# Attention of a streaming encoder: sample values by head on half columns, equal units together, key copies on two engines, both scores taken ahead of the second scaling

## What is computed

```python
# fox: every query block sees all keys up to itself, with a forget term
s = einsum('bqhd,bkhd->bhqk', q_blk, k_all) * ATTN_SCALE
s = s + cq_blk[..., None] - c[:, :, None, :]
s = where(k_pos <= q_pos, s, NEG_INF)
o = einsum('bhqk,bkhd->bqhd', softmax(s), v_all)
# band: a chunk of 64 sees itself and 8 chunks before, with a relative bias
s = einsum('bnqhd,bnkhd->bnhqk', q_ch, k_band) * ATTN_SCALE
s = where(valid, s + bias, NEG_INF)
o = einsum('bnhqk,bnkhd->bnqhd', softmax(s), v_band)
mix = concatenate([o_fox, o_lru, o_band]) @ W_out
```

## Time and profile before

| | |
|---|---|
| three runs, us | 1543.34, 1542.04, 1546.4 (median 1543.34) |
| the profiled execution, us | 1543.2, of which its span is 1541.5 |
| TensorE, VectorE, ScalarE, GpSimd busy, share of the span | 95%, 47%, 30%, 6% |
| attention, from the first key turn to the first matmul of the output projection | 303.1 to 514.7 us of the span |
| chain that ended last, by engine | TensorE 89%, VectorE 6%, ScalarE 2%, issue 1%, DMA 1% |

### The profile page before, as it was taken

The page is one execution under the profiler, slowest core; times in us unless marked ns, Lnnn a source line. Parts: engine busy times, 40 slices in busy tenths (PEclk is TensorE's granted clock), DMA queues, the critical chain, the costliest instruction groups (busy, mean ns, idle before and its releaser), DMA issues.

```text
span 1541.5 us, 20612 instructions
## 1 busy us (share of the span) xinstructions
PE 1461.6 (95%) x8470; PEld 1325.3 (86%) x8470; DVE 728.2 (47%) x1216; ACT 458.4 (30%) x671; POOL 90.7 (6%) x129
## 2 busy tenths in 40 slices
PE   6999999978888899999999999999999999999994
PEld 6999979855666688989898989898989999999993
DVE  6433621166667555553536353535353535444336
ACT  6353332054446543412121212121212221212123
POOL 3000003211000002000000000000000000000006
PEclk9999999989999999999999999999999999999998
DMA  6210212225021323311010111101010101111033
GB/s 206 83 31 35 97 58 108 87 70 190 15 83 55 124 86 106 98 54 55 28 54 27 54 43 39 54 27 54 27 54 27 54 27 54 36 46 52 16 116 135
DMA packets 80005, 102.87 MB, mean 67 GB/s; under 512 B 3592, under 2 KB 63237, under 8 KB 79806
## 3 DMA queue, kind: packets, MB, share of 16 engines
q1 hardware_dynamic: 71744, 73.43, 15.4%
q0 software_dynamic: 8208, 28.69, 5.4%
HBM read 85.52 MB, written 16.58 MB: 66 GB/s over the span
## 4 chain that ended last, share of the span: by engine, by line
PE 89%; DVE 6%; ACT 2%; issue 1%; DMA 1%; POOL 0%; SPq 0%; ACTq 0%; DVEq 0%
PE PS L1423 49%; PE PS L1743 18%; PE PS L1492 7%; PE PS L1710 6%; PE PS L1413 3%; PE PS L1559 2%; PE PS L1665 1%; PE PS L1652 1%; DVE f_acc L1396 1%; DVE probs L1209 1%; PE PS L1498 1%; DVE kt_s L1186 1%; DVE f_acc L1369 1%; PE PS L1582 0%; DMA x_in<-in_x_prompt 0%
## 5 line engine op out<-in xcount | busy, mean ns | idle before, releaser
L1423 PE MATMUL PS<-act_hi,w_hi 128*128 128x384 f32 x1152 | 208.4, 334 | 0.0
L1423 PE MATMUL PS<-act_hi,w_lo 128*128 128x384 f32 x1152 | 207.9, 334 | 0.0
L1423 PE MATMUL PS<-act_lo,w_hi 128*128 128x384 f32 x1152 | 207.9, 334 | 0.0
L1423 PEld LDWEIGHTS PS<-act_hi,w_hi 128*128 128x128 f32 x1152 | 200.8, 188 | 0.9
L1423 PEld LDWEIGHTS PS<-act_hi,w_lo 128*128 128x128 f32 x1152 | 200.4, 188 | 0.0
L1423 PEld LDWEIGHTS PS<-act_lo,w_hi 128*128 128x128 f32 x1152 | 200.4, 188 | 0.0
L1369 DVE TENSOR_TENSOR f_acc<-f_acc,PS 128x512 f32<-128x512 f32 x216 | 145.5, 686 | 77.8 <-PE PS L1743 77.8
L1743 PE MATMUL PS<-w_hi,f_hi 128*128 128x512 f32 x432 | 168.8, 391 | 5.4 <-ACT ffn_rows L977 5.4
L1743 PE MATMUL PS<-w_hi,f_lo 128*128 128x512 f32 x432 | 168.4, 390 | 0.0
L1743 PE MATMUL PS<-w_lo,f_hi 128*128 128x512 f32 x432 | 168.3, 390 | 0.0
L899 ACT ACTIVATE w_hi<-raw 128x1024 fp32r<-128x1024 f32 x72 | 72.1, 1049 | 225.2 <-PE PS L1743 219.5
(11 more groups left out here) (326 smaller groups left out, 2002.9 us busy)
## 6 DMA issues: line engine op xcount, KB each, us to landing
raw<-in_w_up SPq DMA_DIRECT2D x48, 512.0 KB, 4.7
raw<-in_w_down SPq DMA_DIRECT2D x24, 512.0 KB, 3.9
raw<-in_w_in SPq DMA_DIRECT2D x18, 512.0 KB, 4.6
x_scratch<-x POOLq DMA_DIRECT2D x9, 512.0 KB, 5.0
x_back<-x_scratch SPq DMA_DIRECT2D x1, 4608.0 KB, 14.2
x_in<-in_x_prompt SPq DMA_DIRECT2D x8, 512.0 KB, 5.9
raw<-in_w_out SPq DMA_DIRECT2D x8, 512.0 KB, 3.6
x_res<-in_x_prompt SPq DMA_DIRECT2D x8, 512.0 KB, 4.1
```

The lines of the kernel that those rows point to most:

```text
L1423: last = pe.matmul(PS[0:width, banks + c, 0:CW], w(wp, k), acts[ap][:, k, c * CW:(c + 1) * CW], start=(n == 0 and k == 0), stop=(n == 2 an ...
```

## The change

Five things are done together.

- The order of units: fox blocks now come as 5, 7, 6, 4, 3, 2, 1, 0 (before 7, 0, 6, 1, 5, 2, 4, 3), band blocks as 4, 3, 5, 2, 6, 1, 7, 0. Key and sample units stand at given places among them, and the two sample units of a kind no longer follow each other: fox samples at units 21 and 23 (before 22 and 23), band samples at 32 and 37 (before 34 and 35). The splits of output weights begin at unit 37 (before 36) and wait for the scores of the last band sample unit, not for its values.
- Key copies: the second step of a key unit is copied by ScalarE (`take_keys`), the first by VectorE. `scores_used` becomes two semaphores, one for each step.
- VectorE takes both scores of unit m + 2 ahead of the second scaling of unit m + 1.
- Sample values: before, a product gave 128 rows (two heads) by 64 columns (the probabilities of all four heads), of which each head's rows used 16 columns. Now each head has its own product of 64 rows by 16 columns on one half of the array's columns, and the new frames' part is one product of 32 columns for both streams.
- The sample output is copied by one instruction in place of four.

```diff
+        out = []
+        for n in range(len(units) + 1):
+            out += [turn for turn, at in turns if at == n] + units[n:n + 1]
+        return out
...
+    among_fox = list(zip(pairs_of("kb") + pairs_of("kt") + pairs_of("sf"), (9, 11, 12, 14, 15, 16)))
+    among_band = list(zip(pairs_of("kt") + pairs_of("sb"), (4, 5, 6, 10)))
+    units = pairs_of("kf") + with_turns(among_fox, fox) + with_turns(among_band, band)
...
-FOX_ORDER = (7, 0, 6, 1, 5, 2, 4, 3)
-BAND_ORDER = (4, 0, 5, 1, 6, 2, 7, 3)
+FOX_ORDER = (5, 7, 6, 4, 3, 2, 1, 0)
+BAND_ORDER = (4, 3, 5, 2, 6, 1, 7, 0)
...
-OUT_SPLITS = [LAST["sb"] // 2 + 1 + q for q in range(6)]
+OUT_SPLITS = [LAST["sb"] // 2 + q for q in range(6)]
...
+            def take_keys(n):
+                dst, w = keys_of(n)
+                act.wait_ge(scores_ready, n + 1)
+                act.activation(dst, PS[:, 2:4, :].rearrange("p b c -> p (b c)")[:, 0:w], ACT.Copy)\
+                   .then_inc(scores_used[1], 1)
...
                 if q == 0:
-                    act.wait_ge(att_out, outputs_until(LAST["sb"]))
+                    act.wait_ge(scores_ready, LAST["sb"] + 1)
...
+            take_keys(1)
+            take_keys(3)
             for m in range(NUNIT):
...
                 if is_real(m + 2):
                     exponent(2 * (m + 2))
+                elif m + 2 < NUNIT:
+                    take_keys(2 * (m + 2) + 1)
...
                 if m + 2 < NUNIT:
                     take_scores(2 * (m + 2))
+                if is_real(m + 2):
+                    take_scores(2 * (m + 2) + 1)
                 if is_real(m + 1):
                     normalise(COUNT[2 * (m + 1) + 1])
-                if m + 2 < NUNIT:
-                    take_scores(2 * (m + 2) + 1)
...
-                    pe.wait_ge(scores_used, 2 * m + s - 1)
+                    pe.wait_ge(scores_used[s], m)
...
-                                for k in range(3):
-                                    vals = cache_v[:, b, k, t * P:(t + 1) * P] if k < 2 else new[:, NPT, t * P:(t + 1) * P]
-                                    last = pe.matmul(PS[:, bank, c0:c0 + 64], vals,
-                                                     turned[:, k * P + 64 * b2:k * P + 64 * b2 + 64],
-                                                     start=k == 0, stop=k == 2)
+                                for k in range(2):
+                                    for g in range(2):
+                                        col = k * P + 64 * b2 + TS * (2 * t + g)
+                                        pe.matmul(PS[64 * g:64 * g + 64, bank, c0 + TS * b2:c0 + TS * (b2 + 1)],
+                                                  cache_v[:, b, k, t * P + HD * g:t * P + HD * (g + 1)],
+                                                  turned[:, col:col + TS], start=(s, t, b2, k) == (0, 0, 0, 0),
+                                                  stop=False, skip_group_check=True)
+                            for g in range(2):
+                                last = pe.matmul(PS[64 * g:64 * g + 64, bank, c0:c0 + 2 * TS],
+                                                 new[:, NPT, t * P + HD * g:t * P + HD * (g + 1)],
+                                                 new_probs[:, :, 2 * t + g, :], start=False, stop=True,
+                                                 skip_group_check=True)
```

More of the change, by code:

```diff
@@ L133, in with_turns @@
     def with_turns(turns, units):
-        mixed = [x for p, turn in enumerate(turns) for x in (turn, units[p])]
-        return mixed + units[len(turns):]
+        out = []
+        for n in range(len(units) + 1):
+            out += [turn for turn, at in turns if at == n] + units[n:n + 1]
+        return out
     fox, band = prompt("pf", FOX_ORDER), prompt("pb", BAND_ORDER)
-    units = (pairs_of("kf") + fox[:9] + with_turns(pairs_of("kb") + pairs_of("kt"), fox[9:]) + pairs_of("sf")
-             + band[:4] + with_turns(pairs_of("kt"), band[4:8]) + pairs_of("sb") + band[8:])
+    among_fox = list(zip(pairs_of("kb") + pairs_of("kt") + pairs_of("sf"), (9, 11, 12, 14, 15, 16)))
+    among_band = list(zip(pairs_of("kt") + pairs_of("sb"), (4, 5, 6, 10)))
+    units = pairs_of("kf") + with_turns(among_fox, fox) + with_turns(among_band, band)
     return [sub for u in units for sub in u]
-FOX_ORDER = (7, 0, 6, 1, 5, 2, 4, 3)
-BAND_ORDER = (4, 0, 5, 1, 6, 2, 7, 3)
+FOX_ORDER = (5, 7, 6, 4, 3, 2, 1, 0)
+BAND_ORDER = (4, 3, 5, 2, 6, 1, 7, 0)
 STEPS = attention_steps()
@@ L489, in probs_t_of, with keys_of @@
             return ring(r, probs_t, 1)
+        def keys_of(n):
+            st = STEPS[n]
+            if st[0] == "kt":
+                return kt_s[:, 2 * st[1]:2 * st[1] + 2, :, :].rearrange("p b t c -> p (b t c)"), 1024
+            cols, w = (slice(0, SEQ), SEQ) if st[1] < 2 else (slice(SEQ, T), P)
+            return (kt_f if st[0] == "kf" else kt_b)[:, st[1] % 2, cols], w
         def turned_x(t):
@@ L859, in exponent @@
                 r = COUNT[n]
-                act.wait_ge(scores_used, n + 1)
+                act.wait_ge(scores_used[n % 2], n // 2 + 1)
                 p_r = probs_of(r)[:, 0:widths(n)]
@@ L1237, in take_output @@
                     c0 = SEQ + 2 * TS * st[1]
-                    out = PS[:, bank, :].rearrange("p (s t b c) -> p s t b c", s=2, t=2, b=2)
-                    for h in range(H):
-                        t, rows = h // 2, slice(64 * (h % 2), 64 * (h % 2) + 64)
-                        last = dve.tensor_copy(
-                            mix[rows, tile0 + t, c0:c0 + 4 * TS].rearrange("p (s b c) -> p s b c", s=2, b=2),
-                            out[rows, :, t, :, TS * h:TS * (h + 1)])
-                    last.then_inc(att_out_used, 1)
+                    dve.tensor_copy(
+                        mix[:, tile0:tile0 + 2, c0:c0 + 4 * TS].rearrange("p t (s x) -> p s t x", s=2),
+                        PS[:, bank, 0:P].rearrange("p (s t x) -> p s t x", s=2, t=2)).then_inc(att_out_used, 1)
                 else:
@@ L1248, in take_output @@
                                     PS[:, bank, 0:P]).then_inc(att_out_used, 1)
-            for n in range(4):
-                take_scores(n)
+            take_scores(0)
+            take_scores(2)
             for m in range(NUNIT):
@@ L1569, in sample_scores @@
                 kt = kt_f if fox else kt_b
-                pe.wait_ge(scores_used, n - 1)
+                pe.wait_ge(scores_used[s], n // 2)
                 if n == FIRST["sf"]:
@@ L1658, in values @@
                         turned = probs_t_of(2 * v + s)
+                        new_probs = turned[:, 2 * P:3 * P].rearrange("p (b h c) -> p b h c", b=2, h=H)
                         for t in range(2):
+                            c0 = 64 * s + 32 * t
                             for b2 in range(2):
                                 b = 2 * (st[1] + s) + b2
-                                c0 = 256 * s + (2 * t + b2) * 64
-                                for k in range(3):
-                                    vals = cache_v[:, b, k, t * P:(t + 1) * P] if k < 2 else new[:, NPT, t * P:(t + 1) * P]
-                                    last = pe.matmul(PS[:, bank, c0:c0 + 64], vals,
-                                                     turned[:, k * P + 64 * b2:k * P + 64 * b2 + 64],
-                                                     start=k == 0, stop=k == 2)
+                                for k in range(2):
[10 more added lines that the diff above has]
+                                                 skip_group_check=True)
                 last.then_inc(att_out, 1)
```

15 lines of the change are left out of this document (5 added, 10 removed).

## The result

| | us |
|---|---|
| before, 4 runs | 1542.69 (1540.97 to 1546.4) |
| changed kernel, 4 runs | 1502.92 (1501.4 to 1504.33) |
| ratio | 0.9741, 95% interval 0.9725 to 0.9757 |
| predicted | 1517, range 1506 to 1533 |

The kernel became 40 us faster. The direction was right.

What follows compares the result with a forecast made beforehand. Attention was taken as bound by TensorE where units are wide and by the hand-over of score banks elsewhere. Terms 11 + 5 + 4 + 6 + 2 - 3 + 1 = 26 off 1543.2 gave 1517 us, range 1506 to 1533.

Steps and rivals of the forecast that it cites:

- Part 1: Sample values on half columns, four units: 2.4 us each instead of 5.31, counted as 11 us gained.
- first rival: Narrow matmuls in the sample values have a floor per instruction, gaining 1.8 us instead of 11: 1526 us, chance 0.07.
- Part 5: Equal neighbours: fewer waits for turned-back copies where wide units stand beside narrow ones; 2 us gained, bounds 0 and 4.
- part 4: Both score takes ahead of VectorE's second scaling: TensorE waits less for the second take; 6 us gained, bounds 0 and 10.
- Part 6: Narrow fox units (n = 3, 2, 1) in a row: VectorE outlasts TensorE there; 3 us lost, bounds 0 and 6.
- third rival: Waits only move, coming back between narrow units where VectorE is longer than TensorE: 1533 us, chance 0.14.
- Part 2: Attention's start with n = 6 units, not n = 8: first values end earlier; 5 us gained, bounds 2 to 9.
- Part 3: Cached key copies shared between VectorE and ScalarE: TensorE waits less for them; 4 us gained, bounds nothing and 6.
- second rival: ScalarE's key copies come late behind turned-back copies, turning 4 us gained into 6 lost: 1527 us, chance 0.08.
- fifth rival: Clock stays low in the row of narrow units; eight more falls make it slower, 1551 us, chance 0.03.
- fourth rival: More waits close than counted, with no clock fall at the start: 38 us go, 1505 us, chance 0.12.
- The signs that I had set for single parts: Sample values 2.2 to 2.7 us, take waits under 8, key-copy waits about 2, first values ending between 322 and 327.

Runs made afterwards that it cites:

- o_order: Kernel before with only the new order of units, new places of key and sample units and weight splits: 1526.49 us, ratio 0.9891.
- o_start: Kernel before with fox blocks as 5, 0, 7, 1, 6, 2, 4, 3, only the first pair moved ahead: 1544.11 us, ratio 1.0012.
- u_takes: Changed kernel with VectorE's second take of scores put back behind the second scaling: 1506.24 us, ratio to the kernel before 0.9764.
- u_order: Changed kernel with the old order of units, old places, and old begin and wait of the weight splits: 1515.49 us, ratio to before 0.9825.
- u_keys: Changed kernel with both copies of a key unit back on VectorE: 1513.26 us, ratio to the kernel before 0.9798.
- o_values: Kernel before with only the new sample values and their output copy: 1535.44 us, ratio 0.9944.

## Why the prediction was right or wrong

**Part 1, sample values, 11: right.** 2.46 us a unit against 2.4 forecast, 10.9 to 12.1 us in all. 80 instructions in 2.46 us are 31 ns each, so the floor of the first rival did not come. By the Trainium skill's 62 ns with hardware decoding off (TensorE: Matmul & The Clock Gate, section "Back-to-back issue gap") it would have been an estimated 5.0 us. The trace disagrees with that and is near the other floor, about 25 ns, that the same section of the Trainium skill gives.

**Parts 2, 5 and 6, the order, 5 + 2 - 3 = 4: wrong, and this is the step that failed.** Measured 13.8 to 16.5 us at equal clock; the blocks alone gave 10.4 and the places of key and sample units, which had no term, 6.7. The sum went wrong in three places.

- Part 5 booked for unequal neighbours only the waits whose name is the turned-back copy, 5.7 us, and took 2. Most of what unequal neighbours cost stood under another name: the take. Of those 14.9 us I left some 5 to the start and gave the other 10 to part 4, because in the earlier trace rows a scaling lies between two takes and TensorE waits for the second. The scaling was there, but o_order leaves it there and all of these waits fall to 5.8 us. The name in a waits view tells which work came last, not why it came late.
- Part 6 charged 3 us for the narrow units in a row, by comparing VectorE's 1.77 us with TensorE's 1.3 us in one unit. The changed kernel's TensorE waits there in four places of over 0.35 us, 2.9 us in sum (timeline, idle time before each in brackets):

```profile
358.99 0.63 PE L1426 MATMUL PS<-ident,gains 128*128 128x128 f32 x4 [0.50 <-ACT raw L865]
366.59 0.23 PE L1565 MATMUL PS<-cmask_b,ident_b 128*128 128x128 bf16 x1 [0.44 <-ACT kt_s L880]
374.36 0.44 PE L1426 MATMUL PS<-ident,raw 128*128 128x128 f32 x2 [1.26 <-DVE raw L1246]
375.50 0.28 PE L1565 MATMUL PS<-cmask_b,ident_b 128*128 128x128 bf16 x2 [0.70 <-DVE kt_s L1209]
```

  Two of the four are for key copies, and key and sample units stand between the narrow ones, so TensorE has more there than the narrow unit's own 12 instructions. That leaves at most 1.8 us for the narrow units themselves, and the charge was over a microsecond too high. The third rival (waits only move) would have shown there, with over 6 us, and did not come true.
- Part 2 took 5 us for the start. The first values end at 322.8 us, as computed for full clock, and the clock stayed full. But o_start shows that an earlier end, taken alone, is worth nothing: it is no gain unless the work behind it is also done earlier.

**Part 3, key copies, 4: too low.** 6.8 to 7.6 us at equal clock, with the waits for the cached keys down by 4.2 us and those for the new keys, which I had left out. ScalarE's copy came late in two of four cases, by 0.5 and 1.0 us, but TensorE's waits for it stayed at 1.1 us; the second rival, a loss of 6 us, did not come true.

**Part 4, both takes first, 6: too high.** 2.7 to 3.7 us, for the reason given above: most of those waits went with the order. On the old order the edit moves waits to the turned-back copies; on the new one few are left to remove.

**The clock.** I counted it in the start only, and there from 319 us on, although has 0.57 from 312 to 316 us too. It acts in the whole attention: lengths times (1 - clock) give 12.7 us before (211.6 x 0.06) and 3.4 after (170.0 x 0.02), in these two profiled executions. That is not 9 us of gain: over their whole spans the two have 0.987 and 0.989, so the changed kernel had more of its low clock elsewhere. Over all runs the clock goes with about 2 us of the 40. The fifth rival, that the narrow units keep the clock low, did not come: it is 0.99 in that stage.

**The range.** The fourth rival, 38 us off and 1505 us, was the case that came, with a chance of 0.12. Its mechanism was half right: the clock stayed full at the start, but parts 2 to 5 did not reach their far ends as it supposed. The order passed its own, the keys passed theirs by about 1 us, and the takes got 3 of 10. My far ends sum to 11.6 + 9 + 6 + 10 + 4 = 40.6 us, or 1502.6, and the measured time lies there, but that is luck: what the takes did not give, the order gave. The low end was cut at 1506 because all far ends together seemed unlikely; it was too high because the order had been split into small terms with small bounds, 4 us at most for equal neighbours.

The signs that I had set for single parts all came (2.46 us a sample unit, take waits of 3.6 us, 1.8 for cached keys, first values at 322.8 us), and the output projection still began at 472.6 us and not near 489. Those signs said how far each wait should fall, and not which edit would make it fall.

## What to carry to other kernels

Where three engines hand each other banks, order the units so that neighbours are of equal size before touching the order within a unit. Here equal fox blocks side by side were worth about 10 us and the places of the units between them 6 to 7, while the local edit at the very wait that the profile named was worth 3. When a wait has a name, look at the size of the unit ahead of it and behind it, and add up all waits of one cause, whatever engine's name they carry. Read small differences at equal mean clock, beside the difference as measured, and do not book the earlier end of a first stage as a gain until the stages behind it are shown to follow.

## What the hardware showed

- Near-identical kernels had very different stretches of low clock in the attention: length times (1 - clock) was 1.7 to 18.4 us in the profiled executions of the fourteen kernels (a clock of 0.99 in u_takes and u_order, 0.91 in u_keys and o_values). That is one execution of each, so it does not tell kernel from run. A run's time followed its mean clock with 0.8 us for 0.001. What sets off a fall was not settled.
- 128 by 64 weights with 16 moving columns, alternating on the two column halves: 31 ns an instruction over 80 of them (16 of the 80 have 32 columns). The old form, 128 by 128 weights with 64 moving columns, took 111 ns.
- The copy of 1024 columns out of PS took ScalarE 1.03 us and VectorE 1.22 us, side by side.
